# A mixing block with product-key experts and a second block: spread passes, an earlier first dot product, unit 0 decoded in two halves

## The reference, cut to what matters

```
h = rmsnorm(x, g_mix)
z = h @ w_in                                   # 1024 -> 4096: pool, c, b, v, gate_a, gate_b
a = pool_mixer(z_pool) @ w_branch_pool         # mean over the last 2, 4, 8, 16 tokens, minus the token
b = (z_b * conv3(z_c * z_v)) @ w_branch_conv   # causal convolution over three tokens
x = x + (sigmoid(gate_a) * a + sigmoid(gate_b) * b) @ w_out
h2 = rmsnorm(x, g_ffn)
q = h2 @ w_q                                   # 8 heads x 2 halves x 128
s = q . sub_keys                               # 128 scores for each half
top 16 of each half; the 16 x 16 sums; top 16 of those -> idx, gates = softmax
act = gelu(expert_u[idx] . h2)                 # 16 experts for each token and head
x = x + sum(gates * act * expert_v[idx])
```

## Time and profile before

| | us |
|---|---|
| median of 3 runs | 1653.87 |
| lowest, highest | 1649.96, 1662.02 |
| the profiled execution, its own time | 1661.13 |
| its span | 1659.3 |

### The profile page before, as it was taken

How to read it: one execution, slowest core, us unless ns; L and a number is a source line. 1 busy time by engine, 2 the same in 40 slices (tenths; PEclk the granted TensorE clock), 3 DMA queues, 4 the chain that set the end, 5 groups by cost and what they waited for, 6 DMA issues and landing times. The chain is left out here.

```text
span 1659.3 us, 22227 instructions
## 1 busy us (share of the span) xinstructions
PE 1525.0 (92%) x7776; PEld 1146.2 (69%) x7778; DVE 940.4 (57%) x2378; ACT 408.8 (25%) x1003; POOL 599.4 (36%) x524
## 2 busy tenths in 40 slices
PE   8899989989899877777799999999999999999998
PEld 6897945545455333232357788999999878799997
DVE  5742576666766877666455633555552235556554
ACT  2011122222232332222125421211122235311112
POOL 4760234334343343444333103555520000355551
PEclk9999999999999999999999999999997999999999
DMA  8358599999999999999964136545424310545531
GB/s 327 143 208 167 210 386 427 426 426 426 427 423 427 425 427 427 428 427 421 426 261 157 39 138 244 196 153 163 145 101 125 113 66 1 203 156 175 165 126 38
DMA packets 64057, 421.70 MB, mean 254 GB/s; under 512 B 7457, under 2 KB 7905, under 8 KB 18433
## 3 DMA queue, kind: packets, MB, share of 16 engines
q0 software_dynamic: 38944, 277.19, 41.1%
q1 hardware_dynamic: 25024, 143.40, 24.5%
HBM read 416.12 MB, written 3.45 MB: 253 GB/s over the span
## 5 line engine op out<-in xcount | busy, mean ns | idle before, releaser
L2063 PE MATMUL wide<-arena 128*128 128x512 f32 x1024 | 471.6, 607 | 98.2 <-ACT arena L651 97.8
L2063 PEld LDWEIGHTS wide<-arena 128*128 128x128 f32 x1024 | 189.2, 192 | 357.9 <-issue 193.9
L1355 DVE CUSTOM_DVE_ANT_0 arena<-arena,wide 128x1024 f32<-128x1024 f32 x256 | 312.3, 1220 | 178.7 <-DMA arena<-uv_dram,arena 174.2
L494 POOL DMA_INDIRECT arena<-uv_dram,arena x256 | 259.1, 1012 | 406.4 <-PE wide L2063 283.3
L651 ACT ACTIVATE arena<-arena 128x2 f32<-128x2 f32 (+4 forms) x205 | 72.2, 354 | 510.1 <-DVE arena L1355 391.9
L2290 PE MATMUL wide<-arena,wring 128*128 128x256 f32 x704 | 158.6, 379 | 0.0
L1559 DVE SCALAR_TENSOR_TENSOR arena<-arena,prm 128x255 f32<-128x255 f32 (+1 forms) x152 | 125.6, 847 | 56.1 <-ACT arena L651 56.0
L2290 PEld LDWEIGHTS wide<-arena,wring 128*128 128x128 f32 x704 | 130.9, 190 | 16.2
L1593 DVE TENSOR_TENSOR arena<-bank,arena 128x128 f32<-128x128 f32 x266 | 74.0, 290 | 105.0 <-PE bank L2250 101.4
L505 POOL TENSOR_TENSOR arena<-arena 128x512 f32<-128x512 f32 x15 | 20.2, 1346 | 307.0 <-ACT arena L651 306.3
L651 ACT ACTIVATE arena<-bank 128x128 f32<-128x128 f32 (+7 forms) x102 | 41.6, 409 | 355.6 <-PE bank L2250 103.9
(11 more groups left out here) (275 smaller groups left out, 2146.8 us busy)
## 6 DMA issues: line engine op xcount, KB each, us to landing
wring<-ffn_dram SPq DMA_DIRECT2D x44, 1024.0 KB, 5.0
wring<-ffn_dram SPq DMA_DIRECT2D x44, 512.0 KB, 3.5
wring<-win_dram SPq DMA_DIRECT2D x15, 1024.0 KB, 5.2
wring<-wout_dram SPq DMA_DIRECT2D x8, 1024.0 KB, 9.7
wring<-wq_dram SPq DMA_DIRECT2D x5, 1024.0 KB, 7.0
wring<-wout_dram SPq DMA_DIRECT2D x4, 1280.0 KB, 5.6
wring<-mix_dram SPq DMA_DIRECT2D x4, 1024.0 KB, 5.1
arena<-uv_dram,arena POOLq DMA_INDIRECT x256, 11.9
```

The lines of the kernel that those rows point to most:

```text
L494: pool.indirect_dma_start(out=G[:, n % NBUF, :], out_offset=None, in_=a["uv"], in_offset=bass.IndirectOffsetOnAxis(ap=idx[:, u, r:r + 1], ...
L1355: V.tensor_tensor_reduce(out=G[:, n % NBUF, 0:D], in0=G[:, n % NBUF, 0:D], in1=wide[:, 0:2, :].rearrange("p a b -> p (a b)"), scale=1.0, s ...
L2063: ins = MM(wide[:, 2 + h, :], diag[:, n % 4, e, :], G[:, r % NBUF, D + 512 * h:D + 512 * (h + 1)], start=r % (HEADS * TOPK) == 0, stop=r % ...
```

## The change

1. **Passes.** The subtraction of the pool branch is moved behind inverse("mean_mem") and split in four, one for each group (less_itself). beside now does something only behind joins 1, 3 and 5, three operations for each of the twelve slots, 36 in all: the four subtractions, eight memory norms, sixteen steps of the short convolution (its first and its last operation are split in two, so conv_done counts to 2), and the other eight memory norms.
2. **Unit 0's experts.** Its selection searches the places of the first eight, decodes these alone (decode(0), on half the elements), and lets GpSimd start the first eight gathers; only then come the places of the other eight and decode(1). idx_ready therefore counts one more.
3. **Order.** Of unit 1's selection the steps 0 to 3 stay in front of the dot products; steps 4 to 12 follow behind dots 1 to 9 of unit 0, and the selections of units 2, 3 and 4 follow without a break, one step to a dot (up to dot 48). From unit 3 on the steps stand as before. The root, the reciprocal and the normalised input of T1 come later (behind pair 0 on ScalarE; dots 4, 5 and 7 on VectorE), so do the queries of head 3 on TensorE (behind pairs 4 and 6 in place of 2 and 4) and its scores (unit 1, pair 0 in place of unit 0, pair 6). exps(0) stands earlier, exps(1) behind the last pair of unit 0, and exps(2) inside unit 1.

```
...
         def _(pool):
             def gather(u):
-                pool.wait_ge(idx_ready, u + 1)
+                pool.wait_ge(idx_ready, u + 2 if u else 1)
+                    if n == TOPK // 2:
+                        pool.wait_ge(idx_ready, 2)
+                        pool.sem_inc(fence["pool"])
...
             def evict(u, p):
-                if u == 0 and p == 5:
+                if u == 0 and p == 0:
+                    root("mean_ffn1", n=128)
+                    scores_half(2, full("scores_c"))
+                elif u == 0 and p == 7:
+                elif u == 1 and p == 1:
+                    keep_head("scores_3", 3)
+                    exps(2)
...
-                elif u <= 4 and p == 7:
+                elif 1 <= u <= 4 and p == 7:
...
+            exps(0)
-            root("mean_ffn1", n=128)
-            scores_half(2, full("scores_c"))
-            exps(0)
-            exps(1)
             for u in range(UNITS):
...
-                    exps(u + 2)
+                    exps(u + 2 if u else 1)
...
-            V.tensor_tensor(pooled, pooled, zp[0][:, :, 16:16 + S], ALU.subtract).then_inc(pool_done, 1)
+            def less_itself(g):
+                ins = V.tensor_tensor(pooled[:, g, :], pooled[:, g, :], zp[0][:, g, 16:16 + S], ALU.subtract)
+                if g == 3:
+                    ins.then_inc(pool_done, 1)
+                else:
+                    steps(ins)
             def memory_norm(j):
...
             def short_conv(j):
-                if j == 0:
+                if j < 2:
-                    steps(V.tensor_tensor(cu[:, :, 2:2 + S], zc[:, 0:4, :], zc[:, 8:12, :], ALU.mult))
-                elif j < 5:
+                    steps(V.tensor_tensor(cu[:, 2 * j:2 * j + 2, 2:2 + S], zc[:, 2 * j:2 * j + 2, :], zc[:, 8 + 2 * j:10 + 2 * j, :], ALU.mult))
+                elif j < 6:
+                    t = j - 2
-                    steps(V.tensor_scalar(cy[:, j - 1, :], cu[:, j - 1, 2:2 + S], P("conv_w", 3 * (j - 1) + 2), None, ALU.mult))
-                elif j < 13:
-                    tap, t = 1 - (j - 5) // 4, (j - 5) % 4
+                    steps(V.tensor_scalar(cy[:, t, :], cu[:, t, 2:2 + S], P("conv_w", 3 * t + 2), None, ALU.mult))
+                elif j < 14:
+                    tap, t = 1 - (j - 6) // 4, (j - 6) % 4
+                    h = 2 * (j - 14)
-                    V.tensor_tensor(convT, cy, zc[:, 4:8, :], ALU.mult).then_inc(conv_done, 1)
+                    V.tensor_tensor(convT[:, h:h + 2, :], cy[:, h:h + 2, :], zc[:, 4 + h:6 + h, :], ALU.mult).then_inc(conv_done, 1)
             def beside(n, i):
-                if 7 * n + i < 16:
-                    memory_norm(7 * n + i)
-                elif n in (4, 5):
-                    short_conv(7 * (n - 4) + i)
+                j = 3 * n + i // 2
+                if i % 2 == 0:
+                    return
+                if j < 4:
+                    less_itself(j)
+                elif j < 12:
+                    memory_norm(j - 4)
+                elif j < 28:
+                    short_conv(j - 12)
+                else:
+                    memory_norm(j - 20)
             def win_seven(n):
...
-            dve.wait_ge(conv_done, 1)
+            dve.wait_ge(conv_done, 2)
...
+            def decode(q):
+                e = slice(8 * q, 8 * q + 8)
+                oh = [onehot[:, p, :].rearrange("p (k i) -> p k i", k=16)[:, e, :] for p in range(2)]
+                steps(V.tensor_scalar(pij[:, 0, e], pos[:, e], 4, 15, ALU.logical_shift_right, ALU.bitwise_and))
+                steps(V.tensor_scalar(pij[:, 1, e], pos[:, e], 15, 15, ALU.bitwise_and, ALU.bitwise_and))
+                join()
+                for p in range(2):
+                    steps(V.tensor_tensor(oh[p], pij[:, p, e].unsqueeze(2).broadcast_to([128, 8, 16]),
+                                          C("iota", 16).unsqueeze(1).broadcast_to([128, 8, 16]), ALU.is_equal))
+                join()
+                for p in range(2):
+                    steps(V.tensor_tensor(oh[p], oh[p], tif[:, p, :].unsqueeze(1).broadcast_to([128, 8, 16]), ALU.mult))
+                join()
+                for p in range(2):
+                    steps(V.tensor_reduce(eij[:, p, e], oh[p], X, ALU.add))
+                join()
+                V.scalar_tensor_tensor(out=idx[:, 0, e], in0=eij[:, 0, e], scalar=float(NKEYS), in1=eij[:, 1, e],
+                                       op0=ALU.mult, op1=ALU.add).then_inc(idx_ready, 1)
+            def select_in_halves():
+                for step in range(5):
+                    select(0, step)
+                flat, flat_w = cand.rearrange("p a b -> p (a b)"), cw.rearrange("p a b -> p (a b)")
+                join()
+                steps(V.max_index(pos[:, 0:8], fs[:, 0, 0:8], flat))
+                join()
+                decode(0)
+                steps(V.match_replace(flat_w, fs[:, 0, 0:8], flat, -3.0e38))
+                select(0, 6)
+                select(0, 7)
+                join()
+                decode(1)
             def weigh(u):
...
-                    elif u + 2 < UNITS:
+                    elif u >= 3 and u + 2 < UNITS:
+                    at = TOPK * u + r
+                    if u <= 3 and 1 <= at < 49:
+                        select((at + 16) // 13, (at + 3) % 13)
...
-                    if u == 0 and r == 2:
+                    if u == 0 and r == 4:
-                    if u == 0 and r == 3:
+                    if u == 0 and r == 5:
-                    if u == 0 and r == 4:
+                    if u == 0 and r == 7:
...
-            for step in range(13):
-                select(0, step)
+            select_in_halves()
-            for step in range(4, 13):
-                select(1, step)
             for u in range(UNITS):
...
-            pe.wait_ge(conv_done, 1)
+            pe.wait_ge(conv_done, 2)
...
             def between(u, p):
-                if (u, p) in ((0, 2), (0, 4)) or 1 <= u <= 4 and p in (1, 3):
-                    stage, m = f"wq{u + 3}", int(p in (3, 4))
+                if (u, p) in ((0, 4), (0, 6)) or 1 <= u <= 4 and p in (1, 3):
+                    stage, m = f"wq{u + 3}", int(p in (3, 6))
...
-                elif u <= 4 and p == 6:
+                elif u == 1 and p == 0:
+                    pe.wait_ge(freed[ACT_], TAKEN[GROUP0["wq3"]])
+                    score_rows("scores_3", [(3, 0), (3, 1)])
+                elif 1 <= u <= 4 and p == 6:
```

## The result

The changed kernel takes 1651.41 us (median of 20 runs, 1644.82 to 1656.98), the kernel before, run beside it, 1661.82 (20 runs, 1649.96 to 1666.26): a ratio of 0.9949, with a 95% interval of 0.9936 to 0.9962. That is 8.5 us less by the ratio, 6 to 11 by its interval, where 11.7 had been forecast. The forecast time, 1642, missed by more than that, because the three runs it started from had a median of 1653.87 and twenty have 1661.82.

The account below looks back on a forecast made before the run. Gathers at 426 GB/s bound the expert phase, TensorE and VectorE in turn the part before. Win stage 7.2 plus earlier start and filled holes 4.5 gave 11.7 us, from 1653.87 to 1642; range 1635 to 1653.

Parts of the forecast that it names:

- The front: Win stage ahead of the first gather: spreading VectorE's passes over the twelve slots was to save 7.2 us.
- Rival D: Win stage: each spread pass waits out a GpSimd sum, making the kernel 2.3 us slower, 1656; chance 0.05.
- The lower bound: Win stage: every pass at 1.38 us in all twelve slots, 81.3 us against 84.4, saving only 3.1 us.
- P: Estimated time of a win slot, counted from its first product: 4.0 + 2x us, with x one VectorE pass.
- The decode in halves: Unit 0: decoding eight indices first starts the first gather 2.4 us earlier; the rest of VectorE's queue comes 1.6 later.
- The dot products ahead of unit 1's selection: Unit 0: first dot 4.5 us earlier, at 203.9, ninth gather at 212; the DMA hole there closes, returning 3.5 us.
- exps(1): ScalarE, unit 1's first gate: ready 6 us after the dot, behind the last queries' eviction; costed at nothing.
- the lead of the gathers: Expert phase: median 11.9 us from issue to landing against 8.4 with the queue dry; 3.5 us to cover the wait.
- the expert part: Earlier first gather and filled DMA holes in the expert phase, together 4.5 us, from 2.0 to 5.5.
- rival B: Expert phase: exps(1) or TensorE's queries open another hole in unit 1; only 7.2 us gained, 1647; chance 0.17.
- C: Rival for the whole kernel: passes near 0.5, all DMA holes closed, 15 us, up to 18 by clock; 1637; chance 0.15.
- E: Rival: pieces only moved, joins find as much in front, DMA queue drains as before; 0 to 3 us, 1652; chance 0.05.

Follow-up runs that it names:

- e1: The changed kernel with exps(1) moved behind pair 2 of unit 0, out from behind the eviction of head 3's queries; 1648.2 us, ratio 0.9933 to the kernel before.
- e12: The changed kernel itself run once more, nothing altered, on another chip; 1652.9 us, ratio 0.9934 to the kernel before.
- e2: The changed kernel with exps(2) behind pair 5 of unit 1 instead of pair 1; 1650.1 us, ratio 0.9950 to the kernel before.
- e6: The changed kernel with seven of eight matmuls of each of head 4's query products left out; 1647.9 us, ratio 0.9921 to the kernel before.
- e3: The kernel before with the spread passes alone (subtraction in four, three passes to a slot); 1653.4 us, ratio 0.9970.
- e5: e1 plus the second half of unit 0's normalised input written directly behind the first half decode; 1641.4 us, ratio 0.9880 to the kernel before.
- e4: The changed kernel without the spread passes: decode in halves and new order alone; 1659.8 us, ratio 1.0003 to the kernel before.
- e7: The kernel before with seven of eight matmuls of each of head 4's query products left out; 1665.1 us, ratio 1.0008.
- e8: The kernel before with spread passes and decode in two halves, without the new order; 1658.3 us, ratio 0.9967.
- e11: e1 with unit 0 selected and decoded in one piece, as before; 1653.2 us, ratio 0.9918 to the kernel before.
- e9: e5 with head 3's queries two dot products earlier, and the half normalisation they need at dots 3 to 5; 1646.4 us, ratio 0.9909 to the kernel before.
- e10: e5 with exps(2) behind pair 5 of unit 1 instead of pair 1; 1650.3 us, ratio 0.9920 to the kernel before.

## Why the prediction was wrong, step by step

**The front: right.** Forecast 7.2, measured 7.3. TensorE's rows at the first product of the second slot, at the longest stand that is left between slots, and at the bias matmuls:

```profile
46.84 1.06 PE L1879 MATMUL bank<-hT,wring 128*128 128x128 f32 x8
...
72.66 1.13 PE L1879 MATMUL bank<-hT,wring 128*128 128x128 f32 x8 [0.39 <-DVE arena L1227]
...
117.07 1.67 PE L1914 MATMUL bank<-arena,prm 33*12 33x512 f32 x4
```

The stand of 2.04 us in the earlier trace rows is gone. Slot 0 took 6.91 (forecast 7.1), slot 1 6.25 (6.4), slots 4 and 5 13.13 (12.7), the eight others 0.7 over 6.27 each in all (0.8). One slot, 65.85 to 72.66, took 6.81, just over the 6.7 that I had set. In slot 0 TensorE waited 0.39 us for one of GpSimd's sums, the tenths that were allowed for them. VectorE by form, 39.9 to 117 us, against the earlier trace rows:

```profile
L1227 DVE TENSOR_TENSOR arena<-bank,arena 128x128 f32<-128x128 f32 x83 | 21.9, 283 | 25.6 <-PE bank L1879 25.5
L1182 DVE SCALAR_TENSOR_TENSOR arena<-arena,prm,rstd 128x256 f32<-128x256 f32 x16 | 13.2, 822 | 0.0
L1198 DVE SCALAR_TENSOR_TENSOR arena<-arena,prm 128x256 f32<-128x256 f32 x8 | 7.8, 975 | 0.0
...
L1173 DVE TENSOR_TENSOR arena<-arena 128x256 f32<-128x256 f32 x4 | 2.9, 728 | 0.0
L1190 DVE TENSOR_TENSOR arena<-arena 128x512 f32<-128x512 f32 x2 | 2.8, 1424 | 0.0
```

And two rows of before, 39.9 to 124.3, which the earlier trace rows doesn't have, the convolution's additions and its first product:

```profile
L1185 DVE SCALAR_TENSOR_TENSOR arena<-arena,prm 128x256 f32<-128x256 f32 x8 | 6.8, 853 | 0.0
...
L1178 DVE TENSOR_TENSOR arena<-arena 128x1024 f32<-128x1024 f32 x1 | 1.6, 1622 | 0.0
```

The norms average 0.822 where I took 0.96, the four subtractions 0.73 where I took 1.38. Rival D needed 1.70 and is refuted: the 36 passes average 0.88. The norms got shorter, but the convolution's additions (0.975 for 0.853) and its first product (2.8 us in two halves for 1.6) got longer; all passes together take 31.8 us, and took 31.0 before. So the gain is not that spread passes are cheaper; it fits what the prediction had, that only two of them stand in front of the join that TensorE waits for. (The lower bound had a slip: twelve slots with P = 6.76 are 81.1 us, not 81.3.) The Trainium skill (SBUF — State Buffer, "SBUF: two separate sides") says that a VectorE operation with two inputs in SBUF and one of GpSimd's lock each other out for a whole instruction. The trace agrees in kind, with passes of 0.47 and of 0.98 to 1.09 us in one slot (62.7 to 65.9); the worst case that the prediction drew from it, a whole sum waited out by every pass, didn't come.

**The decode in halves: right.** The first gather was forecast 9.6 us earlier and came 9.7 earlier; the rest of VectorE's queue was to be 1.6 later and was 186.48 against 191.78 - 7.3 = 184.5, so 2.0. GpSimd's rows against the earlier trace rows:

```profile
183.21 1.13 POOL L497 DMA_INDIRECT arena<-uv_dram,arena  x1 [13.55 <-issue]
...
205.81 1.01 POOL L497 DMA_INDIRECT arena<-uv_dram,arena  x1 [12.26 <-PE wide L2122]
```

**The dot products ahead of unit 1's selection: nearly.** The first dot product was forecast 11.7 earlier and came 10.0 earlier, the ninth gather 12.5 and came 11.4. From the start of VectorE's queue to unit 1's first maximum it took 7.8 us for 6.3, by as much as TensorE's 24 matmuls behind its gap of 2.85 took longer (4.61 for 3.06). Had they not, ScalarE might have stood instead: in e1 they took 3.07, its eviction stood until 11.5 us after the first gather, and the first dot product came at 199.0. The late first dot product cost nothing that shows: the stream was full from 192 to 240, which is above the 420 GB/s that I had asked for, and the expert matmuls came at 2.4 GHz (eight in 3.70) as assumed.

**exps(1): the step that failed.** "It is costed at nothing; without that cover it takes 2 of the 4.5." Both halves were wrong for the changed kernel. I set the wait against "the lead of the gathers", 3.5 us. But the lead was that of landings ahead of use. What the wait delays is use, hence the freeing of buffers, and VectorE stood 5.57 us, more than the lead and more than TensorE's backlog. Then I let TensorE stand "only 2 us" and took those for the price. TensorE stood 2.58, ran the next eight matmuls at the lower clock in the changed kernel and in e12 (1.70 more), and the lateness stayed. Price: 4.4 us by e1, 5.5 by the hole in the stretch; where the matmuls behind the gap kept the higher level (e2, e6), some 2. If the front's 7.3 reach the end, the expert part's gain was 6.2 - 7.3 = -1.1, not 4.5, and with exps(1) early 10.6 - 7.3 = 3.3. Against e3, whose front brought only 4.1 to the last dot product, it is 2.1 and 6.5.

The prediction had this outcome as rival B, whose condition ("the exps(1) wait ... opens another one in unit 1") is what came, at 0.17. At the last dot product B gives 7.2 and 6.2 was measured. My own mark against the forecast, "DMA holes in unit 1 of over 2 us", was met by one of 5.5. The case for B was on the page: TensorE 85% busy over the phase as a mean, and 28.75 of 29.71 us, 97%, in the stretch where unit 0's queries are on top. I named only the mean. (e6 doesn't bear out, though, that a lighter TensorE would have kept the gain.)

**The base: the larger part of the missed time.** "The median of the runs shown is 1653.87, 7.3 below, so 1642 for the median." The profiled 1661.13 was close to the median of twenty, 1661.82; the 7.3 us were an accident of three runs. The measured time is 9.4 us above the forecast: 8.0 of it is the base (1661.82 for 1653.87), 1.3 the sum (11.7 against a difference of the medians of 10.4; against the ratio's 8.5 it is 3.2). That the difference of the medians, 10.4, comes so near the 11.7 is in part luck: the mechanism missed a cost of over 4 us. Where the accident seems to come from is a stage that the change leaves alone, the compression of the second layer. TensorE there, its 64 matmuls of 128x68, in the changed kernel and in e5:

```profile
1258.09 13.92 PE L2395 MATMUL bank<-arena 128*128 128x68 f32 x64
```

```profile
1253.12 7.82 PE L2397 MATMUL bank<-arena 128*128 128x68 f32 x64
```

The mean granted clock from 1250 to 1300 is 0.80 in the first and 1.00 in the second: 1.2 GHz for part of the stretch. The kernel before has 13.92 in its profiled execution as well. From the mixing matmuls ahead of it to those behind the stage, before took 1262.10 to 1287.17, 25.1 us, and e5 1252.05 to 1267.69, 15.6. Of the 60 runs of before beside the experiments, 22 are between 1652 and 1659 and 38 between 1662 and 1668, with none between, medians 1656.2 and 1664.4. Two of the three runs I was given fell among the lower. The changed kernel shows the same less sharply: its 26 runs, parted by the mean clock of the execution at 0.989, have medians of 1649.6 (12) and 1654.1 (14), 6.6 and 10.3 below the groups of before (which are parted by time, so the two divisions are not quite alike). The spread sits behind the expert phase: from the last dot product to the end of the span it is 805.5 to 807.6 us in the six profiles with 13.92 in the stage (before, changed, e4, e7, e8, e11) and 794.6 to 799.5 in six of the eight with 7.82; the other two, e1 and e12, have 803.1 and 803.0, with a lower clock in 860 to 900 and 1300 to 1400 (0.91 and 0.95). So e5's 0.9880 is not to be read as 20 us of mechanism. The profile of before (1661.13) is also 3.3 us below the median of its slower group, that of the changed kernel (1656.98) 2.9 above its own, so the 4.2 us between them, and perhaps the 6.2 at the last dot product, understate the gain; how much of the ratio's 8.5 is which, the runs don't say. That the stage's level makes the two groups of times is inferred, since each profile shows one execution.

**Rivals.** B's mechanism came, C's holes closed except for the new one (e1 is the nearest, 10.6 of 15), D and E are refuted: passes averaged 0.88, and each moved piece moved.

## What to carry to other kernels

When a small operation of a side engine is moved behind a wait, price it by the whole chain behind it: who uses its result, what that user frees, and which transfer waits for what is freed. If the transfers already run at their full rate, take it that a hole in them isn't made up later (4.4 us lost at 240 were still lost at 843), and don't set such a wait against the time by which they land ahead of use. A start made earlier by 9.7 us is worth only what the first freed buffer follows it by (e8's profile: nothing), so follow the ninth transfer and not the first. And take the base of a forecast from the execution in which the durations were read, unless many runs say otherwise: here the three runs shown lay 8 us below the twenty.

## What the runs showed of the hardware

- The same TensorE stage ran at either clock level in different executions of nearly the same program: 64 matmuls of 128x68 in 13.92 us (six profiles, before and changed among them) or 7.82 (eight, e1, e5 and e12 among them), 9.4 us over the stretch around it.
- Behind a gap of 2.58 us eight matmuls of 128x512 took 5.40 us (changed, e4, e12) or 3.70 (e2, e6). Behind one of 2.85 us 24 matmuls of 128x128 took 4.53 to 5.49 (changed, e4, e6, e8, e12), and 3.07 in e1 and e2. The gap was the same each time, the level wasn't.
- In eleven of the fourteen profiles an engine goes on 11.4 to 11.7 us after the first gather was issued, although the matmuls that it waits for by the program had been through for some time: ScalarE's eviction of head 1's scores in e1, e2, e4, e5, e8, e9, e10 and e12 (0.8 to 3.7 us after the scores), VectorE's last addition for T1 in e3, e7 and e11 (after standing 2.3 to 2.5). TensorE's stops without a releaser in e3, e5, e7 and e11 end then too, or 1.4 us earlier. Query loads and gathers fill the DMA queue at that time. The cause was not tried.
- VectorE passes beside GpSimd's sums, spread against in a row: norms 0.822 us on average for 0.957, the convolution's additions 0.975 for 0.853, all of them 31.8 us for 31.0.
